# Both FFNs and both output projections as seven block products in place of eight, their inputs passed through DRAM

## What is computed

```
x = x + mlstm_mixer(rmsnorm(x, a_norm[l]), ...)      # ends in  h.astype(x.dtype) @ w_out     (1024 x 1024 x 1024)
x = x + swa_sink_mixer(rmsnorm(x, b_norm[j]), ...)   # ends in  o @ w_out + b_out            (1024 x 1024 x 1024)

def swiglu(x, w_gate_up, w_down):
    gu = x @ w_gate_up                               # 1024 x 1024 x 5632
    g, u = jnp.split(gu, 2, axis=-1)
    return (jax.nn.silu(g) * u) @ w_down             # 1024 x 2816 x 1024
x = x + swiglu(rmsnorm(x, ffn_norm[l]), w_gate_up[l], w_down[l])
```

## Time and profile before

| | |
|---|---|
| time, three runs | 2269.93 to 2271.94 us, median 2271.89 |
| profiled execution, first to last instruction | 2268.2 us (3.7 us less than the median: start and end of the execution) |
| PE busy | 2229.7 us, 98% |
| DVE, ACT, POOL busy | 1000.8, 566.3, 347.0 us (44%, 25%, 15%) |
| DMA | 114.17 MB, 50 GB/s |

### The profile page before, as it was taken

One profiled execution on the slowest core, in us unless ns is written; L12 is line 12 of the kernel. 1 busy time (PEld: TensorE's weight loads), 2 busy tenths in 40 slices (PEclk: granted clock), 3 DMA queues, 4 the chain that ended last, 5 costly groups with the idle time before them and its releaser, 6 DMA issues.

```text
span 2268.2 us, 28010 instructions
## 1 busy us (share of the span) xinstructions
PE 2229.7 (98%) x10704; PEld 1852.8 (82%) x10704; DVE 1000.8 (44%) x1769; ACT 566.3 (25%) x1163; POOL 347.0 (15%) x226
## 2 busy tenths in 40 slices
PE   7999999999999999999999999999999999999998
PEld 6898997888888888888887777788888888888887
DVE  7433335743333334333455778674333332333334
ACT  5323323231111111111133555323111111111112
POOL 4222003221111111111115002112111111111100
PEclk9999999999999999999999999999999999999999
DMA  5211122111111111111121000011111111111101
GB/s 131 85 56 56 37 65 102 56 38 47 46 55 46 46 46 46 55 46 46 55 47 38 20 20 20 25 60 38 47 47 55 46 46 46 53 49 46 46 28 74
DMA packets 158987, 114.17 MB, mean 50 GB/s; under 512 B 30008, under 2 KB 146760, under 8 KB 158928
## 3 DMA queue, kind: packets, MB, share of 16 engines
q1 hardware_dynamic: 156208, 103.89, 15.6%
q0 software_dynamic: 1568, 5.29, 0.7%
q10 hardware_dynamic: 1152, 4.19, 0.5%
HBM read 109.14 MB, written 4.23 MB: 50 GB/s over the span
## 4 chain that ended last, share of the span: by engine, by line
PE 94%; DVE 4%; ACT 1%; issue 1%; SPq 0%; DMA 0%; POOL 0%; DVEq 0%; POOLq 0%; ACTq 0%
PE ps L1285 55%; PE ps L1287 27%; PE ps L1568 2%; PE ps L1413 1%; PE ps L1416 1%; PE ps L1417 1%; PE ps L1605 1%; PE ps L1607 1%; PE ps L1344 1%; DVE X L936 1%; PE ps L1589 1%; DVE x_normed L918 1%; PE ps L1463 1%; PE ps L1468 1%; PE ps L1474 0%
## 5 line engine op out<-in xcount | busy, mean ns | idle before, releaser
L1285 PE MATMUL ps<-xT_hi,w_hi 128*128 128x512 f32 x1840 | 730.2, 397 | 0.0
L1285 PE MATMUL ps<-xT_lo,w_hi 128*128 128x512 f32 x1840 | 717.9, 390 | 0.0
L1287 PE MATMUL ps<-xT_hi,w_lo 128*128 128x512 f32 x1840 | 573.4, 390 | 0.0
L936 DVE TENSOR_TENSOR X<-ps,X 128x512 f32<-128x512 f32 x464 | 303.3, 687 | 381.5 <-PE ps L1287 381.2
L484 POOL TENSOR_TENSOR raw<-raw,gain_cols 128x1024 f32<-128x1024 f32 x123 | 243.7, 1985 | 1238.1 <-DMA raw<-in_w_gate_up_dram 1132.9
L1285 PEld LDWEIGHTS ps<-xT_hi,w_hi 128*128 128x128 f32 x1840 | 345.5, 188 | 83.9 <-issue 13.9
L1287 PEld LDWEIGHTS ps<-xT_hi,w_lo 128*128 128x128 f32 x1840 | 345.6, 188 | 72.4
L1285 PEld LDWEIGHTS ps<-xT_lo,w_hi 128*128 128x128 f32 x1840 | 346.0, 188 | 69.1
L898 DVE TENSOR_TENSOR w_lo<-raw,w_hi 128x1024 fp32r<-128x1024 f32 x183 | 237.7, 1302 | 334.3 <-ACT w_hi L612 334.3
L612 ACT ACTIVATE w_hi<-raw 128x1024 fp32r<-128x1024 f32 x183 | 189.6, 1053 | 513.3 <-PE ps L1285 481.1
L1285 PE MATMUL ps<-w_hi,hidden_hi 128*128 128x512 f32 x768 | 300.6, 391 | 0.0
(11 more groups left out here) (156 smaller groups left out, 1847.2 us busy)
## 6 DMA issues: line engine op xcount, KB each, us to landing
raw<-in_w_gate_up_dram SPq DMA_DIRECT2D x88, 512.0 KB, 3.8
raw<-in_w_down_dram SPq DMA_DIRECT2D x44, 512.0 KB, 3.2
raw<-in_a_w_in_dram SPq DMA_DIRECT2D x24, 512.0 KB, 4.3
X<-in_x_dram SPq DMA_DIRECT2D x8, 512.0 KB, 5.1
raw<-in_a_w_out_dram SPq DMA_DIRECT2D x8, 512.0 KB, 3.4
X<-in_x_dram ACTq DMA_DIRECT2D x8, 512.0 KB, 6.5
raw<-in_b_w_q_dram SPq DMA_DIRECT2D x16, 256.0 KB, 3.6
raw<-in_b_w_out_dram SPq DMA_DIRECT2D x16, 256.0 KB, 3.6
```

Source lines behind the costliest of these rows:

```text
L936: dve.tensor_tensor(xv, ps[:, b, :], xv, ALU.add).then_inc(bank_free[b], 1)
L1285: ms_ = [mm(ps[:, b + half, :], ah, t[:, c[half]], start=start and t is bh, stop=False) for half in halves for t in (bh, bl)]
L1287: ms_ += [mm(ps[:, b + half, :], al, bh[:, c[half]], start=False, stop=stop) for half in halves]
```

## The change

Every matrix product of the two FFNs and the two output projections is cut into 2x2 blocks and computed by seven block products (Winograd's form) in place of eight. For C = A B with blocks A11..A22 and B11..B22 it uses A11, A12, A22 and four sums of A's blocks, and B11, B21, B22 and four sums of B's blocks. Each of these fourteen forms is split into hi and lo. The seven products accumulate in three PSUM banks; a bank is read by DVE or ACT between two products that add to it, and the next product on the bank waits for that read.

The work is cut into 46 items a layer, written out without loops, with 7 products each:

- 8 items of the output projection (2 chunks of k by 4 token groups): a product is 2 k-tiles x 3 passes = 6 matmuls of 512 columns.
- 22 items of the FFN's gate and up part (one hidden tile each): 4 k-tiles x 3 = 12 matmuls a product. The split x^T forms stay resident in `forms`; the weights are streamed into `mats`.
- 16 items of the down part (4 chunks of k, of 3, 3, 3 and 2 row pairs, by 4 token groups): 9 or 6 matmuls a product. Here the weight rows are resident in `forms` (four slots) and the hidden activations are streamed.

The streamed side is always a raw buffer, four POOL sums, seven ACT copies into `mats` (hi) and seven subtractions (lo, three on DVE, four on POOL); `mats` has one buffer, so that form q of the next item is written once product q of this item is done. The resident side of a row pair is four POOL sums of 128x512, seven ACT copies and seven DVE subtractions. Mixer outputs and hidden tiles are stored to DRAM and loaded back by token group; X is spilled to DRAM after the norm and reloaded before the down part. The gain of the FFN norms is applied to the tokens (L1488), not to the weights. `first_output_pair`, `end_of_norm` before the FFNs and before K/V, and the loops of the FFN go.

```diff
+NQ = 7
+BANK_OF = (0, 2, 0, 1, 0, 2, 0)
+OPENS = (True, True, False, True, False, False, False)
+PLAIN_A = {0: 0, 3: 1, 6: 2}
+SUM_A = {1: 0, 2: 1, 4: 2, 5: 3}
+PLAIN_B = {0: (0, 0), 3: (1, 0), 5: (1, 1)}
+SUM_B = {1: 0, 2: 1, 4: 2, 6: 3}
...
+            def bank_is_read(it, q):
+                before = items[it.n - 2] if local(it) >= 2 else None
+                if OPENS[q] and before is not None:
...
+                if q in (2, 4, 5, 6):
...
+                    else:
+                        done, count = d_add, NQ * down_no[it.n] + {2: 1, 4: 3, 5: 2, 6: 5}[q]
+                    pe.wait_ge(done, count)
+            def product(it, q):
+                operands(it, q)
+                bank_is_read(it, q)
...
+                for k in range(w):
...
+                    mm(dst, ah, bh, start=OPENS[q] and k == 0, stop=False, skip_group_check=True)
+                    mm(dst, ah, bl, start=False, stop=False, skip_group_check=True)
+                    m = mm(dst, al, bh, start=False, stop=k == w - 1, skip_group_check=True)
+                m.then_inc(prod, 1)
...
+            def stream_sums(it):            # POOL
...
+                pool.tensor_tensor(s[0], a21, a22, ALU.add).then_inc(ssum, 1)
+                pool.tensor_tensor(s[2], a11, a21, ALU.subtract)
+                pool.tensor_tensor(s[1], s[0], a11, ALU.subtract).then_inc(ssum, 2)
+                pool.tensor_tensor(s[3], a12, s[1], ALU.subtract).then_inc(ssum, 1)
+            def stream_lo(it, q):           # POOL for q in SUM_A, DVE for q in PLAIN_A
...
+            def run(l):                     # DVE
+                for it in its:
...
+                    for q in range(NQ):
+                        if it.up:
+                            up_out(it, q)
+                        else:
+                            add_product(it, q)
+                        for q2 in refill_after(it, q):
+                            if q2 in PLAIN_A:
+                                stream_lo(its[i + 1], q2)
+                        for r, f in forms_after(it, q):
+                            row_lo(r, f)
+                        if it.seam:
+                            norm, g = it.seam
...
+                            if q == 6:
+                                if norm % 2 and g:
+                                    quarter_lo(norm, g - 1, (2, 3, 4))
+                                mean_square_of(norm, g, 0)
+                                if norm % 2 and g:
+                                    quarter_lo(norm, g - 1, (5, 6))
+                                mean_square_of(norm, g, 1)
...
+                                for e in range(2):
+                                    x_normed_of(norm, g, e)
+                    if l == 0 and i == 0:
+                        gate_head(NH_A - 1, last=True)
```

More of the change, by code:

```diff
@@ new lines, in refill_after, with refill_needs @@
+    def refill_after(it, q):
+        nxt = items[it.n + 1] if it.n + 1 < len(items) else None
+        if nxt is None or nxt.layer != it.layer:
+            return []
+        if it.cold:
+            return {5: [0, 1, 2], 6: [3, 4, 5, 6]}.get(q, [])
+        if it.width == 2 and nxt.width == 4:
+            return {1: [0], 3: [1], 5: [2]}.get(q, [])
+        return [q]
+    def refill_needs(it, q):
+        before = items[it.n - 1]
+        return NQ * before.n + (min(2 * q + 1, 6) if before.width == 2 and it.width == 4 else q) + 1
@@ L162, in yoco_kernel, with local, stream_buffer, row_arrived @@
+    def local(it):
+        return it.n - runs[it.layer][0].n
+    def stream_buffer(it):
+        return 2 + local(it) if local(it) < 2 else it.n % 2
+    stream_total, stream_arrived = [0] * 4, {}
+    for it in items:
+        stream_total[stream_buffer(it)] += 32 if it.up else 16
+        stream_arrived[it.n] = stream_total[stream_buffer(it)]
+    def row_arrived(r):
+        if r.part == "out":
+            return (16, 48)[r.layer]
+        return 16 * (r.layer + 1)
     x2 = x[0]
@@ new lines, in load_row @@
+            def load_row(r, f):
+                dst, loaded = raw_of(r)[f], row_loaded[r.index % (4 + FP)][f]
+                ft = 2 * r.number + f
+                if r.part == "out" and r.layer == 1:
+                    for a in range(2):
+                        r0 = (a * PAIRS + ft) * DH_B
+                        sp.dma_start(dst[a * DH_B:(a + 1) * DH_B, :], w_out[1][r0:r0 + DH_B, :]).then_inc(loaded, 16)
+                else:
+                    w = w_out[0] if r.part == "out" else wdn[r.layer]
+                    sp.dma_start(dst[:], w[ft * P:(ft + 1) * P, :]).then_inc(loaded, 16)
@@ L422, in _ @@
+            for j in range(2):
+                sp.wait_ge(y_gated, 2 * j + 2)
+                store_y(0, 2 * (NH_A - 1) + j, yh[:, j, :], y_stored[j])
+            run(0)
+            for j in range(2):
+                sp.wait_ge(prod, NQ * last_of_run[0].n + Unit(U_KV + j).raw + 1)
+                load_cols(Unit(U_KV + j), wkv[:, :, j * P:(j + 1) * P])
             for u in range(PAIRS):
@@ L723, in head @@
                 for c in range(TT):
-                    if c % 4 == 0:
+                    if c % 4 == 0 and not last:
                         write_hi(un[4 + c // 4] + LEAD)
@@ L818, in _ @@
-            ffn(0, 2)
+            run(0)
+            act.wait_ge(prod, NQ * (last_of_run[0].n + 1))
+            for j in range(LEAD):
+                write_hi(Unit(U_KV + j))
             for j in range(2):
@@ L947, in down_and_norm, with row_lo @@
[L947 to L960 removed]
+            def row_lo(r, q):
+                dve.wait_ge(rhi, form_no[r.index, q])
+                dve.tensor_tensor(forms[:, r.slot, q, 1, :], row_source(r, q), forms[:, r.slot, q, 0, :].bitcast(F32),
+                                  ALU.subtract).then_inc(rlo, 1)
@@ L1172, in _ @@
-            ffn(0, 2)
+            run(0)
+            for j in range(LEAD):
+                write_lo(Unit(U_KV + j))
             write_lo(Unit(U_KV) + LEAD)
```

1202 lines of the change are left out of this document (803 added, 399 removed).

## The result

| | before | after |
|---|---|---|
| median, us | 2270.9 (2269.8 to 2271.9, 4 runs) | 2376.5 (2370.6 to 2376.8, 4 runs) |
| span of the profiled execution, us | 2268.2 | 2368.9 |
| mean granted TensorE clock | 0.993 | 0.946 |

The change makes the kernel 4.6% slower: ratio 1.046, 95% interval 1.0445 to 1.0475. The forecast was 2254, with a range of 2145 to 2345. The prediction was wrong in its sign and outside its range.

What follows compares the result with a forecast made beforehand. PE bound the kernel: number of matmuls times their pace. 35.1 - 31.7 - 20 + 47.8 - 42.8 = -11.6, corrected by +10 and -16, made span 2250.6; with 3.7 around it, 2254 us, range 2145 to 2345.

Steps and rivals of the forecast that it cites:

- the rule of exclusion: Everywhere: POOL's operations and DVE's with both inputs in SBUF exclude each other for a whole operation; additions from PSUM don't wait.
- the next item's first addition comes 8.4 after the last product, its third product 5.8 late: Output projection items 4 to 7: squares, copies, quarter forms and two scalings stand ahead of the next item's first addition.
- 15.4: Output projection items 4 to 7, with the norm: total waits in us per layer, 1.0 + 2.8 + 5.8 + 5.8.
- into gate and up 9.5: From output projection to gate and up: 10.6 us to the first product, 1.1 of it transposes, so 9.5 of wait.
- 8.1: Down items 42 to 45, with the norm: third product 2.7 us late, three times.
- 8.7: Layer 0, from down into K/V: 9.8 us after the last product against 3.3 before, 1.1 of it transposes.
- five places of 2: Correction of +10 us: five more waits where PE sets the pace, each losing about 2 us at half clock.
- My rival: Down part: PE falls to half clock once in each of 32 items, 2 us each, giving 2318; chance 0.14.
- the sum that I drew from that page: Forecast with the reference page's POOL times: about 69.4 us exclusive time per chunk of four, some 37 us higher in all.
- The sign that I had named: Down part: the forecast is wrong where PE waits for POOL and not for DVE.
- 23.8 + 8.5: End of attention without `first_output_pair`: seven steps of 3.4 us and a drain of 8.5, 17.1 us less.
- the -16: Correction for row items: POOL busy 75%, so a quarter of DVE's waits, 1.6 us in each of ten items, goes.

Runs made afterwards that it cites:

- Runs 5: The changed kernel with eight block products again in the two down projections alone: 2302.6 us.
- runs 6: The changed kernel with eight block products again in the two output projections alone: 2328.0 us.
- run 7: The changed kernel with eight block products in both output and both down projections, seven only in gate and up: 2255.6 us, ratio 0.9942 to the kernel before.
- 9: Seven products in gate and up alone, with norm scalings ahead of most quarter forms and ACT's first square one product earlier: 2248.9 us, ratio 0.9907 to the kernel before.
- experiment 2: The changed kernel with extra matmuls where PE waits: product 1 repeated in items 0, 5 to 7, 43 to 45, single matmuls ahead of 30, 34, 38: 2345.5 us.
- 11: Seven products everywhere, scalings first and next item's additions ahead of or between quarter forms, plus extra matmuls ahead of items 30, 34, 38: 2340.0 us, 2337.3 without them.
- experiment 4: The changed kernel with GpSimd's subtractions for the low halves cut to one column, PE reading the high half instead: 2316.4 us.

## Why the prediction was wrong

By its own steps; "missed by" adds both layers and is in us of the profiled executions. It comes to the 111.6 of the table above, within 3 (items 1 to 4 are within 2 each); the corrections (-16 + 10) and 0.7 at the ends make it the 118.3 between 2250.6 and 2368.9.

| step | forecast | measured | missed by |
|---|---|---|---|
| gate and up, items 9 to 28 | 19.0 each | 19.0 each | 0 |
| entry into output projection A | 7.6 | 7.7 | 0 |
| item 0 | 15.7/14.5 | 19.9/16.1 | +6 |
| items 5 to 8 with the way into gate and up | 81.7/80.0 | 106.7/107.3 | +52 |
| item 30, with the wait ahead | 27.1 | 25.8/26.2 | -2 |
| item 31 | 17.5 | 24.9/23.9 | +14 |
| items 33, 35, 37, 39, 41 | 16.3 | 15.8 four times, 14.3 | -8 |
| items 34 and 38, with the wait ahead | 20.7 | A 24.0, 23.2; B 23.5, 24.0 | +12 |
| items 42 to 45, A with the way into K/V | 63.5/46.2 | 77.0/58.2 | +26 |
| K/V and attention | 255.5 | 267.4 | +12 |

- **Right: what goes, and gate and up.** The matmuls and their pace came out as worked out, and no engine of the new work stopped PE in 20 items a layer, though GpSimd's operations there took 1.43 us in the mean and not 1.20. Runs 5 to 7 and 9 show that this is the part to keep.
- **Right: the rule of exclusion for single instructions.** DVE's scaling took 2.27 beside GpSimd and 1.27 alone, its subtractions into `forms` beside a busy GpSimd 1.15 to 1.24 in the mean against 0.69 of the additions, which stayed at 0.69. The items beside a row pair ran at 15.8 or less, under the 16.3 of the forecast. The Trainium skill (SBUF — State Buffer, "SBUF: two separate sides") says that of a DVE operation with two SBUF inputs and a GpSimd operation that reads SBUF the one that starts first has their shared port for its whole instruction, and the other waits. The rows agree, down to a one-column operation (0.55 to 1.52).
- **The failed step: the items with a norm** ("the next item's first addition comes 8.4 after the last product, its third product 5.8 late", "15.4", "into gate and up 9.5", "8.1", "8.7"). They hold 78 of the 112 us. The addition came 10.4 after the last one. I had counted ACT's and DVE's operations, and neither the waits between them at each hand-over (0.2 to 1.35 us, several in a row) nor GpSimd's power at 1.52 and its quarter subtractions beside the scalings. Item 6 of layer A shows what this made: its third product came 8.2 us late and not 5.8, eleven matmuls behind that wait ran at half clock (2.2 us), and PE waited 1.3 more ahead of the next transposes. One step was missing wholly: item 8, which I took at 19.0, takes 26.3/24.9, since the copy of its first product stands on ACT behind the quarter forms (the wait of 4.15 above).
- **Mis-sized: half clock.** I gave it 10 us, five places of 2. The mean clock of 0.946 is 256 us at the lower level against 32 before ((1 - 0.946) x 2 x 2368.9, and (1 - 0.993) x 2 x 2268.2). What it cost is less than the slow matmuls suggest, and it depends on the place: 31 us in the items with a norm (experiment 2), nothing measurable ahead of items 30, 34 and 38 (11), and 6.3 in attention's last steps between runs 6 and 7. My rival put it in all 32 down items; of these only those with a norm are shown to have paid. Its premise, a fall behind every wait above 2 us, does not hold in the changed kernel: behind a wait of 2.22 us the clock fell in item 2 of layer A and not in item 3, and in layer B it fell behind neither 2.32 nor 2.91.
- **Mis-sized: GpSimd's price and its queue.** Alone its operation took 1.27, 1.01 and 0.73 us for 512, 384 and 256 columns; I took 1.20, 0.92 and 0.63, and said that 1.0 at 384 would eat the gain (3 us over 44 operations are 0.07 each, not 0.08; the 1.0 stands). An estimate from the GPSIMD Engine Reference of the Trainium skill (Elementwise, side by side) had been 1.33, 1.07 and 0.81: the measured ones lie between, and the sum that I drew from that page was 37 us higher. But the place was another: the items beside rows stayed below my figure, and the excess came at items 31, 34 and 38, where the row sums queue behind four stream sums. The sign that I had named, PE waiting for POOL in the down part, holds for these (the rows of item 31, and experiment 4).
- **Mis-sized: attention, with the clock there put at nothing.** The last seven steps and the drain took 42.7 us where 23.8 + 8.5 was forecast. That most steps took near 3.4 is luck: 3.4 was the pace with other matmuls between a step's own; without them a step takes 2.3 to 2.7 at full clock (run 7, one even 1.9), and 3.6 is its pace at half clock, at which the changed kernel runs from 1474.6 to the projection. Two of the first steps, beside GpSimd's row sums, took 4.0 (before the clock fell) and 5.5, and the drain 16.2 in place of 8.5. That run 7's attention comes to 254.3 with 255.5 forecast is luck as well: its steps are shorter than I took them and its drain, 14.9, longer.
- **Partly right: the -16** for waits in items with rows where GpSimd is idle: the five plain ones came out 8 under their figure in the two layers, half of it in item 41, which shows no wait at all (14.3).

What stays open: K/V and attention took 267.4 us in the changed kernel, and 262.1 and 254.3 in runs 6 and 7, which have no row sums there. Between the last two, the time at half clock is what differs (37 and 15 us; 49 in the changed kernel). How the other 5 us divide between GpSimd's row sums and the still earlier fall of the clock was not tried, and neither was what the passing through DRAM alone costs.
